# Routing reordered, loads and stores moved to SyncE, and the closing norm's sums taken from the combine

## The reference, cut to what matters

```python
for l in range(DEPTH):
    m = chunk_gmlp(x, ...) if l == 0 else diff_head_merge(diff_attn(x, ...), ...)
    x = layer_norm(ALPHA * x + m, ln1_g[l], ln1_b[l])
    x = layer_norm(ALPHA * x + grouped_moe(x, router_w, router_bias, w_up[l], w_down[l]), ln2_g[l], ln2_b[l])

def grouped_moe(x, router_w, router_bias, w_up, w_down):
    probs = softmax(x @ router_w); sel = probs + router_bias
    # best group of 4 experts by its two best, then the two best experts in it; gates normalised
    for e in range(16):
        gate, up = split(x @ w_up[e]); out += combine[..., e] * ((silu(gate) * up) @ w_down[e])
```

## Time and profile before

| what | us |
|---|---|
| three runs | 1332.38, 1335.71, 1339.65 |
| median | 1335.71 |
| the profiled execution, its own time | 1342.47 |
| its span, first to last instruction | 1340.4 |

### The profile page before, as it was taken

The page is one execution under the profiler, slowest core; times in us unless marked ns, Lnnn a source line. Parts: engine busy times, 40 slices in busy tenths (PEclk is TensorE's granted clock), DMA queues, the critical chain, the costliest instruction groups (busy, mean ns, idle before and its releaser), DMA issues.

```text
span 1340.4 us, 16767 instructions
## 1 busy us (share of the span) xinstructions
PE 1138.3 (85%) x5868; PEld 883.2 (66%) x5868; DVE 918.0 (68%) x1037; ACT 687.2 (51%) x738; POOL 268.5 (20%) x266
## 2 busy tenths in 40 slices
PE   5987996899999998269999998779589999999820
PEld 4765675678888887146777666567567888888710
DVE  4456567788888888673442565656778888888844
ACT  4233233477777777322211465522347777787711
POOL 3011036241111110240000100003524111112223
PEclk9998896899999999678999998879689999999965
DMA  9220256489999997651332234225648999999641
GB/s 341 104 91 6 100 192 229 171 284 369 373 369 368 379 378 284 239 191 65 128 135 89 92 129 158 100 94 208 241 147 280 378 372 370 367 378 374 232 157 67
DMA packets 142543, 302.57 MB, mean 226 GB/s; under 512 B 11888, under 2 KB 12064, under 8 KB 142368
## 3 DMA queue, kind: packets, MB, share of 16 engines
q1 hardware_dynamic: 123008, 250.23, 52.4%
q0 software_dynamic: 19200, 51.33, 10.5%
q10 hardware_dynamic: 288, 0.39, 0.1%
HBM read 288.40 MB, written 30.28 MB: 238 GB/s over the span
## 4 chain that ended last, share of the span: by engine, by line
PE 42%; DVE 7%; DMA 2%; ACT 2%; issue 1%; POOL 0%; SPq 0%; DVEq 0%; POOLq 0%; ACTq 0%; PEldq 0%
PE ps L1572 11%; PE ps L1574 11%; PE ps L1573 11%; DVE x L1356 1%; PE ps L1938 1%; DVE wl L952 1%; PE ps L1919 1%; PE ps L1838 1%; PE ps L1595 1%; PE ps L1685 1%; PE ps L1955 1%; ACT wh L670 1%; PE ps L1777 1%; DMA raw<-in_cache_k 1%; DMA xg<-x_rows,gidx 1%
## 5 line engine op out<-in xcount | busy, mean ns | idle before, releaser
L952 DVE TENSOR_TENSOR wl<-raw,wh 128x2048 fp32r<-128x2048 f32 x210 | 479.2, 2306 | 206.9 <-ACT wh L670 203.1
L670 ACT ACTIVATE wh<-raw 128x2048 fp32r<-128x2048 f32 x210 | 398.1, 1915 | 182.4 <-PE ps L1595 86.1
L1572 PE MATMUL ps<-wh,xgTh 128*128 128x512 f32 x512 | 209.1, 408 | 6.3 <-DVE xgTl L1304 5.7
L1573 PE MATMUL ps<-wl,xgTh 128*128 128x512 f32 x512 | 205.0, 400 | 0.0
L1574 PE MATMUL ps<-wh,xgTl 128*128 128x512 f32 x512 | 204.6, 400 | 0.0
L1572 PE MATMUL ps<-wh,xTh 128*128 128x512 f32 x384 | 159.4, 415 | 15.6 <-DVE u L1021 10.6
L1574 PE MATMUL ps<-wh,xTl 128*128 128x512 f32 x384 | 154.6, 403 | 0.0
L1573 PE MATMUL ps<-wl,xTh 128*128 128x512 f32 x384 | 154.6, 403 | 0.0
L1572 PEld LDWEIGHTS ps<-wh,xgTh 128*128 128x128 f32 x512 | 97.7, 191 | 35.3 <-DVE wl L952 7.4
L1572 PE MATMUL ps<-wh,hTh 128*128 128x512 f32 x256 | 105.9, 414 | 10.4 <-DVE hTl L1315 10.4
L1574 PEld LDWEIGHTS ps<-wh,xgTl 128*128 128x128 f32 x512 | 97.7, 191 | 23.8
(11 more groups left out here) (267 smaller groups left out, 1628.8 us busy)
## 6 DMA issues: line engine op xcount, KB each, us to landing
raw<-in_moe_w_up SPq DMA_DIRECT2D x120, 1024.0 KB, 9.7
raw<-in_moe_w_down SPq DMA_DIRECT2D x62, 1024.0 KB, 10.9
raw<-in_a_w_in SPq DMA_DIRECT2D x8, 1024.0 KB, 20.8
ahead_up<-in_moe_w_up SPq DMA_DIRECT2D x8, 1024.0 KB, 12.1
yl<-y_rows POOLq DMA_DIRECT2D x8, 1024.0 KB, 9.4
raw<-in_cache_k SPq DMA_DIRECT2D x16, 512.0 KB, 4.4
raw<-in_cache_v SPq DMA_DIRECT2D x16, 512.0 KB, 5.4
raw<-in_a_w_out SPq DMA_DIRECT2D x4, 1024.0 KB, 5.0
```

The costliest lines, as they stand in the source:

```text
L670: act.activation(wh[:, slot], src, ACT.Copy).then_inc(high[key], 1)
L952: dve.tensor_tensor(wl[:, slot], src, wh[:, slot].bitcast(F32), ALU.subtract).then_inc(low[key], 1)
L1572: pe.matmul(out, high_, w_high, start=start, stop=False)
L1573: pe.matmul(out, high_, w_low, start=False, stop=False)
```

## The change

What it does, by parts:

1. **Tail of the routing tiles.** PE transposes tile n-1 between the two halves of tile n's projection and multiplies it with the router's weights behind tile n, so only one tile is left behind the last projection. ACT copies before it takes the last root. POOL no longer applies gain and shift to tile 4: DVE does, in two operations over the whole tile, ahead of the routing.
2. **First chunk of layer 1's experts** is split during the tiles (as layer 0's was) and no longer between the lists and `route_rest`.
3. **End of `route_rest`** (table, gates, the extra lists; now `route_end`) moves behind the second gathered tile on DVE; PE reads the table later. The extra lists' matmuls on PE move behind the first gathered tile's transpose. The 48 filling transposes become 36, and 8 more stand ahead of block 0's first matmul.
4. **No more `ahead` buffers.** Block 1's chunks go through the `raw` slots like all others.
5. **Rows of the experts** are read back by SP and not by POOL; **the result is stored** by SP, each tile when it is ready.
6. **Closing norm of each layer.** DVE's second combine delivers the row sum with it; ACT sums the squares of x minus mean (a Square with an accumulated output); the two half-tile statistics and their aggregation on DVE go. The last tile's gain moves from POOL to DVE.

The diff, cut to its core:

```diff
-GAINED = [0, TILES - 1, 2 * TILES - 1, 3 * TILES - 2, 4 * TILES - 2]
-WARM_TURNS = 48
+GAINED = [0, TILES - 1, 2 * TILES - 2, 3 * TILES - 4, 4 * TILES - 5]
+OUTS = [0, TILES, 2 * TILES - 1, 3 * TILES - 1, 4 * TILES - 2]
+WARM_TURNS, MORE_TURNS = 36, 8
...
# SyncE
-                sp.wait_ge(proj_done, (M_ROUTE_B if l else M_ROUTE_A) + 1)
-                sp.wait_ge(vs_out, 16)
-                for q in range(4):
-                    sp.dma_start(ahead_up[q][:], chunk(a["moe_w_up"][l, 1], q % 2, q // 2)).then_inc(ahead_in[q], 16)
-                sp.dma_start(ahead_down[:], down_chunk(a["moe_w_down"][l, 1], 0)).then_inc(ahead_in[4], 16)
+                up(l, 1, 1, previous(1))
                 up(l, 2, 2, previous(2))
                 down(l, 1, 1, previous(1))
...
+            def fetch(l, blocks):
+                landed, turned = sp.to_reg(16 * blocks), sp.to_reg(blocks + 1)
+                sp.wait_ge(plan, l + 1)
+                sp.wait_ge(moe[l]["scattered"], landed)
+                sp.wait_ge(moe[l]["xg_low"], turned)
+                pairs = y_rows[l].rearrange("(k n) d -> n k d", k=2)
+                for t in range(TILES):
+                    sp.dma_start(yl[0:ROWS[t], t], dram_tile(t, pairs)).then_inc(y_in[t], 16)
...
+            fetch(1, blocks)
+            for t in range(TILES):
+                sp.wait_ge(ln_out, OUTS[4] + t + 1)
+                sp.dma_start(out_tile(y_tiles, t), x[0:ROWS[t], t]).then_inc(y_out, 16)
...
# ScalarE, closing norm
+            def spread(call, t):
+                m = ROWS[t]
+                act.wait_ge(z_mean, TILES * (call // 2 - 1) + t + 1)
+                act.activation(yl[0:m, t, 0], x[0:m, t], ACT.Square, bias=zsum[0:m, 1, t:t + 1],
+                               accum_out=zsum[0:m, 2, t:t + 1]).then_inc(z_spread, 1)
+            def ln_tiles(call, t0=None, whole=False):
                 for i in range(TILES + 3):
+                    if 0 < i <= TILES:
+                        normalise(call, i - 1, x)
+                    if i < TILES:
+                        spread(call, i)
+                    if i >= 3 and t0 is not None:
                         turn_high(t0 + 2 * (i - 3), i - 3, whole=whole and i - 3 == SAMP)
...
# VectorE, closing norm
                 for i in range(TILES + 3):
                     if i < TILES:
-                        produce(i)
-                        ln_stats(call, i, x)
+                        add(i, 0)
+                    if 0 < i <= TILES:
+                        dve.wait_ge(z_spread, TILES * (call // 2 - 1) + t + 1)
+                        dve.tensor_scalar(lns[0:m, 0, t:t + 1], zsum[0:m, 2, t:t + 1], 1.0 / D, EPS, ALU.mult, ALU.add
+                                          ).then_inc(ln_var, 1)
+                    if i < TILES:
+                        add(i, 1)
+                    if 0 < i <= TILES:
+                        ln_scale(call, i - 1)
                     if 0 <= i - 2 < TILES:
                         ln_shift(call, i - 2, x)
-                    if i < TILES:
-                        ln_scale(call, i)
...
# VectorE, add(t, 1)
+                        link(dve.scalar_tensor_tensor(out=w, in0=yl[0:m, t, 1], scalar=gate, in1=w,
+                                                      op0=ALU.mult, op1=ALU.add, accum_out=zsum[0:m, 0, t:t + 1]))
+                        dve.tensor_scalar(zsum[0:m, 1, t:t + 1], zsum[0:m, 0, t:t + 1], -1.0 / D, None, ALU.mult
+                                          ).then_inc(z_mean, 1)
...
# VectorE, routing tiles: the last tile's gain and shift
+                dve.wait_ge(gb_in, 16 + 32 * call)
+                dve.wait_ge(tr_done, t0 + 2 * TILES)
+                last = x[:, TILES - 1]
+                link(dve.scalar_tensor_tensor(out=last, in0=last, scalar=mv[:, TILES - 1, 0:1], in1=gb[:, 0:D],
+                                              op0=ALU.subtract, op1=ALU.mult))
+                dve.scalar_tensor_tensor(out=last, in0=last, scalar=lns[:, 2, TILES - 1:TILES], in1=gb[:, D:2 * D],
+                                         op0=ALU.mult, op1=ALU.add).then_inc(last_out, 1)
...
                 route(l, m0)
-                if l:
-                    split(0, 0, 0, 0)
-                route_rest(l)
+                incl = route_rest(l)
...
                 gate_up(0)
                 xg_low(1)
+                route_end(l, incl)
...
# TensorE
+                def amid(n):
+                    pe.wait_ge(proj_free, w0 + n)
+                    turn(n - 1, t0 + 2 * (n - 1), x[:, n - 1])
                 def behind(n):
-                    if n:
-                        pe.wait_ge(proj_free, w0 + n)
-                        turn(n - 1, t0 + 2 * (n - 1), x[:, n - 1])
-                    if n > 1:
-                        logits(n - 2)
-                    if n == TILES:
-                        logits(TILES - 1)
+                    logits(n - 1)
...
                 turn_x(0)
+                route_extra(l)
+                warm_turns(MORE_TURNS)
                 up(0, 0)
```

More of the change, by code:

```diff
@@ L330, in prompt_tile, with out_tile @@
             return ap[(t - 1) * P:t * P]
+        def out_tile(rows, t):
+            return rows[1] if t == SAMP else prompt_tile(t, rows[0])
         def chunk(w, kh, cb):
@@ L360, in down @@
             def down(l, e, i, slot_free):
-                for r in range(1 if isinstance(i, int) and i == 1 else 0, 2):
+                for r in range(2):
                     slot_free(4 + r)
@@ L373, in free @@
                         if slot < 4:
-                            sp.wait_ge(low_m, (slot if isinstance(i, int) and i == 2 else 6 * (i - 1) - 2 + slot) + 1)
+                            sp.wait_ge(low_m, (slot if isinstance(i, int) and i == 1 else 6 * (i - 1) - 2 + slot) + 1)
                         else:
@@ L450, in _ @@
                 if c == 4:
+                    fetch(0, blocks)
                     sp.wait_ge(y_in[TILES - 1], 16)
@@ L618, in _ @@
             v_rows = [v_prompt[0].rearrange("s h d -> s (h d)"), v_sample.rearrange("b t h d -> (b t) (h d)")]
-            def out_tile(rows, t):
-                return rows[1] if t == SAMP else prompt_tile(t, rows[0])
             for cb in range(2):
@@ L770, in split @@
                 def split(n, slot, q, i):
[L772 to L778 removed]
+                    split_high(key, n, (slot + l) % SPLIT_SLOTS, raw[:, q], raw_m[l][q], 16 * (i + 1))
                 for n in range(begun, 3):
@@ L932, in _ @@
             split_b(15)
-            ln_routed(1, 3, T_LN1B, None)
-            moe_act(1, [16, 14, 15], "b")
-            for t in range(TILES):
-                normalise(4, t, x)
+            ln_routed(1, 3, T_LN1B, split_early(1, [14, 15, 16], "b"))
+            moe_act(1, [14, 15, 16], "b", 1)
+            ln_tiles(4)
         @block.vector
@@ L1291, in split @@
                 def split(n, slot, q, i):
-                    if isinstance(i, int) and i == 1 and q < 5:
-                        split_low(key, n, slot, (ahead_up[q] if q < 4 else ahead_down)[:])
-                    else:
-                        split_low(key, n, slot, raw[:, q])
+                    split_low(key, n, (slot + l) % SPLIT_SLOTS, raw[:, q])
                 route(l, m0)
-                if l:
-                    split(0, 0, 0, 0)
-                route_rest(l)
+                incl = route_rest(l)
                 def xg_low(i):
@@ L1728, in project_by_tile @@
                             mm.then_inc(used[key], 1)
+                        if kh == 0 and amid:
+                            amid(n)
                     begun = True
@@ L1825, in up @@
                     for q in range(4):
-                        slot = (q + 1) % 3 if n0 else q % 3
+                        slot = (q + l + (1 if n0 else 0)) % SPLIT_SLOTS
                         pe.wait_ge(low[key], (6 * i - 2 + q if n0 else q) + 1)
```

189 lines of the change are left out of this document (94 added, 95 removed).

## The result

The changed kernel takes 1314.62 us (median of four runs, 1312.34 to 1317.35) against 1334.05 for the kernel before in the same comparison: a ratio of 0.984, with a 95% interval from 0.9815 to 0.9866. The prediction, 1311.5 in a range from 1298 to 1327 and faster, holds. Its steps hold less well than its number: two of them missed by 3.4 and 5.1 us in one direction, and two more by 2.0 and 5.0 in the other.

The account below looks back on a forecast made before the run. PE bounds the kernel and is full in mid-expert blocks, so only routing heads and closing norms can move. Gains 7.9 + 7.7 + 2.0 + 6.6 = 24.2 us; against 1335.71 that gives 1311.5, range 1298 to 1327.

Parts of the forecast that it names:

- the tail: End of the kernel: the 8 us between the last store's landing and the span's end were left unchanged.
- layer 0's norm: Closing norm after layer 0: gain 2.0 us, bounds -2 and 5, ACT's later transpose copies giving much back.
- Head of the routing: Start of each layer's experts: DVE no longer held by POOL, net gain 2.8 us, less a 2.0 PE stall in layer 1.
- The gather: First gather of each layer lands in 4.3 us without the `ahead` loads: gain 2.8 in layer 0, 4.6 in layer 1.
- TensorE's clock: Block 0's first 14 matmuls run at the upper clock level: gain 2.8 us in each layer, bounds 0 and 2.8.
- Rival 1: Clock falls all the same as PE waits for the gathered tile's split: 5.6 us back, 1317.1; chance 0.19.
- The end of `route_rest`: Ahead of block 0's hidden rows on DVE: 14 small operations, 3.4 us, 5.6 cover; loss 0.5 per layer, 3.4 without cover.
- Rival 2: Routing head: tile 3's POOL pair holds DVE's new pair, up to 9.4 us lost, 1320.9; chance 0.14.
- Rival 3: Closing norms: the combine that delivers a sum runs at half speed, 1.30 us more each, 1322.5; chance 0.10.
- Rival 4: Experts without prefetch: DMA engines become the bound, 11.6 us slower, 1347.3; chance 0.07.
- The closing norm: After layer 1: fewer DVE statistics save 1.2 us for each of four tiles, 4.8; taken as 3.0.
- near 5: Sign of being right: one tile of the closing norm takes near 5 us on DVE, from 6.08.

Follow-up runs that it names:

- e6: The kernel before, unchanged, profiled a second time: span 1333.2 us, its run 1335.39 us.
- e9: Changed kernel with tile 4 of both routed norms normalised by ACT and scaled and shifted by POOL again, DVE's new pair removed: 1312.40 us.
- e3: Changed kernel plus one small POOL memset that waits for the last tile's shift: span 1315.0 us.
- e4: Changed kernel with the five 1 MB loads per layer put back at their old place, into buffers nobody reads: 1318.55 us, one run.
- e10: Changed kernel with layer 1's tile 0 transposes behind tile 1's whole projection instead of in its middle: layer 1's routing head 50.25 us, from 50.6.
- e11: Changed kernel with `route_end` spread over three places, closing norms without POOL, and e10's edit: 1301.87 us, 0.973 of the kernel before.
- e12: e11 plus ten turns of PE where it idled ahead of block 0's hidden rows: 1296.65 us, 0.9705 of the kernel before.
- e5: Changed kernel without the 8 turns behind the extra lists, the 36 kept: 1316.51 us.
- e2: Changed kernel with DVE instead of POOL multiplying all tiles by gamma in both closing norms: 1303.22 us, 0.9758 of the kernel before.
- e7: Kernel before with only the last five stores and the waits for all stores moved from POOL's queue to SP's: last shift to end 6.0 us, from 14.3.

## Why the prediction was right, and where its steps were not

**The sum was right through errors that cancel, so by luck.** 24.2 us were forecast. In the stretches that the change touches, the traces show 24.1 (the table's 21.4 without the -0.2 and -2.5 of the start and the attention), give or take the 1.5 by which block 1 moves in each layer. Of the steps, 8.5 us too much stood in blocks 0 and 1, against 5.0 and 2.0 too little in the tail and in layer 0's norm and some 1.4 in smaller rows. The number came out 3 us low all the same, as the medians moved by 19.4: in the two stretches that the change doesn't touch the profile after is 2.7 us longer than the second before, and they vary by 6 from run to run (e6).

**Head of the routing: right.** 2.8 forecast, 2.8 measured in layer 0, and e9 gives 2.1 and 2.0 of it back by restoring POOL's pair in place of DVE's. The net of 0.8 in layer 1 was right in this profile (0.8), with a stall of 1.83 for the 2.0; where the clock fell behind the stall, the head took 1.5 more (e3, e4). The 2.0 can't be had back by order alone: e10, e11 and e12 took the stall away and gained 0.4 to 0.8.

**The gather: right,** 2.8 and 4.6 forecast, 3.4 and 4.6 measured, and landing in 4.0 and 4.2 us; e4 shows the loads as its cause, in layer 1 for 3.2 of 4.6.

**TensorE's clock: right for block 0, and not followed further.** The step said "I take the clock as held: 14 x 0.203 = 2.8 in each layer". Block 0's up fell from 13.9 to 11.5 us in layer 0 and from 13.5 to 11.5 in layer 1 (second profile), so 2.4 and 2.0, and e5 shows that the eight turns do it. But in the changed kernel eight matmuls of block 1 ran at the lower level, 1.6 us back in each layer, and seven to thirteen did in every profile that keeps `route_end` in its new place. Rival 1 ("the clock falls all the same") was true one block later.

**The end of `route_rest`: the step that failed.** "14 small operations of at most 0.24, 3.4 us", with 5.6 us of cover, "a loss of 0.5". The size of the step was wrong. The 14 operations took 5.25 us, where the kernel before does the same 14 in 2.85 at their old place (235.55 to 238.40): the first five were stretched beside POOL's first scaling and the start of its second. And the register load, which stood in the shade of DVE's operation in the kernel before, now follows them and adds 1.05 (0.80 in layer 1). So 6.3 and 6.0 passed, and PE's 25th matmul came 2.08 and 3.36 us behind the 24th, instead of 0.23. How much of the 5.6 was free can be had from that: with the clock up until the wait, PE lost 3.1 of the 6.0 in layer 1, and in e2's layer 0 3.4 of 6.3, so 2.9 were free. ACT's half of the split, `h_low` and DVE's half of 2.29 use the rest. At 3.4 the step would have cost the 0.5 that was forecast, though the prediction shows no working for that 0.5. The other 1.6 in each layer is the clock. I had named the work that hides the step, but not what would hold it in its new place.

**Rival 2 was right in kind and wrong in place.** Where the two meet, POOL can hold DVE. The head is free of it (DVE's pair starts 0.5 us behind POOL's last operation there and takes 1.28 and 1.28), but `route_end` (up to 1.60 for a small copy) and the second combine of two closing tiles (3.18 and 3.03 instead of 1.28) are not. The Trainium skill ("SBUF — State Buffer", "SBUF: two separate sides") tells of one pair of ports that VectorE and GpSimd lock for a whole instruction, the other waiting, for VectorE's instructions with two SBUF inputs and for some of its faster modes. The traces agree in part: the combine of 3.18 us ended 1.08 behind POOL's operation, POOL's own took 4.36 instead of 2.35 just before, and copies with one input were slowed as well. But `route_end`'s later operations ran freely beside POOL's second scaling, one with two inputs in SBUF among them (0.32 us, as in the kernel before), so not every meeting costs.

**Rival 3 is refuted.** With the sum the combine takes 1.28 us and 0.08 for the read of the accumulator, so the Trainium skill's line on halved throughput ("Vector Engine (DVE) Microarchitecture Reference", 7. Points that are easy to get wrong) doesn't hold for this instruction here.

**Rival 4 is refuted:** late blocks take 18.2 us, and PE never waits for a transfer in them; block 1, whose chunks were the prefetched ones, takes its 11.5 us without them in e12.

**The closing norm.** At the end, 3.0 forecast and measured, though not as worked out: a tile in the middle still takes 6.06 us (1287.33 to 1293.39), not "near 5", since POOL's hold of 1.9 ate the saving; the gain came from the first tiles, and e2 has the 5.4. After layer 0 the term of 2.0 measured 4.0: I took it that ACT's copies of the transposes would give much back, and PE reached tile 2 without losing any.

## What to carry to other kernels

A step moved into the shade of other work needs two checks: what already uses that shade, and which engine's operations it will meet in its new place; here 2.85 us of small operations became 6.3 with a register load, and of a cover of 5.6 only 2.9 were free. Where VectorE's path counts, POOL's help can cost more than it saves: its three multiplications spared DVE 3.7 us and held it for as long, and the norm was 2 us longer than with DVE alone. And look at the last instructions of every engine, the sequencers' included, before calling the end of a kernel fixed.

## What the runs showed of the hardware that was not expected

- POOL's closing drain ends 9.5 us behind POOL's last operation in the changed kernel and in every kernel made from it, e2 too, where that was 34 us earlier and so cost nothing. In the kernel before, where POOL first waits for the stores, it took 7.4 from their landing, and in e7 it ended 7.0 behind POOL's last operation.
- The same wait does not always cost TensorE its upper level. Ahead of block 0 it held in all twenty places with a wait of 1.21 us (the changed kernel and its edits but e5) and fell in all eight with 2.14 (e5) or 2.37 (the kernel before, e6, e7). Ahead of block 1, with waits of 1.31 and 0.48, it fell in ten places of twenty (and in none of six in the kernel before, e6 and e7, whose block 0 had begun at the lower level). Where it held there and PE then waited for the third chunk (3.36 to 3.63 us between two matmuls), it fell behind that wait, in eight of eight.
- Of VectorE and GpSimd either can be the one that is held: GpSimd's multiplication took 4.36 us instead of 2.35 beside a shift and a combine, and the next combine 3.18 instead of 1.28 (the changed kernel).
- A VectorE operation that delivers a row sum costs no more than one that doesn't (1.28 us for 1024 columns, and 0.08 for the read), where such a read on ACT takes 0.21.
